# Seven half-size products for each pair of feed-forward up tiles, and the down product as a second pass

## The reference

```
h = rmsnorm(x, g_ffn)
u = h @ w_up                                   # (1024, 1024) @ (1024, 5632)
f_gate = causal_dwconv(u[:, :2816], conv_f_w) + conv_f_b      # 3 taps over tokens
f = gelu(f_gate, tanh) * u[:, 2816:]
x = x + f @ w_down                             # (1024, 2816) @ (2816, 1024)
```

## Time and profile before

| | us |
|---|---|
| median of 3 runs (lowest to highest) | 2121.4 (2120.72 to 2123.34) |
| the profiled execution | 2123.06 |
| its span, first to last instruction | 2121.3 |
| mean granted clock of PE | 0.985 |
| feed-forward part: first up product to last down product | from 619.6 to about 1380 |

### The profile page before, as it was taken

One profiled execution on the slowest core, in us unless ns is written; L12 is line 12 of the kernel. 1 busy time (PEld: TensorE's weight loads), 2 busy tenths in 40 slices (PEclk: granted clock), 3 DMA queues, 4 the chain that ended last, 5 costly groups with the idle time before them and its releaser, 6 DMA issues.

```text
span 2121.3 us, 24908 instructions
## 1 busy us (share of the span) xinstructions
PE 2048.5 (97%) x9765; PEld 1705.9 (80%) x9765; DVE 1177.4 (56%) x1119; ACT 438.5 (21%) x547; POOL 730.0 (34%) x534
## 2 busy tenths in 40 slices
PE   6999999999999999999999999999899999999998
PEld 5888788887887888888888888878788878888877
DVE  4999995313436655566556655744433745556520
ACT  4000001302222000000000000233222235555411
POOL 2444354454232343333433333423122511112221
PEclk9999999999999999999999999999799989999999
DMA  4211111232131112221122112211123210000033
GB/s 134 60 42 48 40 44 45 74 105 60 40 107 52 60 50 80 69 68 38 62 79 69 52 42 74 79 30 40 30 74 95 75 41 1 11 11 1 1 129 90
DMA packets 176851, 122.08 MB, mean 58 GB/s; under 512 B 8771, under 2 KB 160272, under 8 KB 176784
## 3 DMA queue, kind: packets, MB, share of 16 engines
q1 hardware_dynamic: 175504, 118.77, 18.5%
q10 hardware_dynamic: 1280, 2.35, 0.3%
HBM read 112.71 MB, written 8.39 MB: 57 GB/s over the span
## 4 chain that ended last, share of the span: by engine, by line
PE 79%; DVE 7%; issue 4%; POOL 4%; DMA 4%; ACT 3%; SPq 0%; POOLq 0%; DVEq 0%; ACTq 0%
PE ps L488 67%; POOL wlo L437 2%; DMA raw<-in_w_up 2%; PE ps L872 2%; POOL whi L435 1%; DVE prob L1864 1%; PE ps L905 1%; PE ps L886 1%; PE ps L889 1%; PE ps L883 1%; PE ps L907 1%; PE ps L906 1%; PE ps L880 1%; PE ps L892 1%; PE ps L697 1%
## 5 line engine op out<-in xcount | busy, mean ns | idle before, releaser
L437 POOL TENSOR_TENSOR wlo<-raw,whi 128x1024 fp32r<-128x1024 f32 (+2 forms) x162 | 458.4, 2830 | 13.5
L434 POOL TENSOR_TENSOR small<-ones 128x1 f32<-128x1 f32 x166 | 50.7, 306 | 1123.5 <-PE ps L488 928.3
L488 PE MATMUL ps<-xb_hi,whi 128*128 128x512 f32 x1216 | 381.0, 395 | 15.9 <-POOL wlo L437 4.3
L488 PE MATMUL ps<-xa_hi,whi 128*128 128x512 f32 x1184 | 373.8, 395 | 7.6 <-DVE xa_lo L1604 3.1
L488 PE MATMUL ps<-xb_lo,whi 128*128 128x512 f32 x1216 | 376.6, 391 | 0.0
L488 PE MATMUL ps<-xb_hi,wlo 128*128 128x512 f32 x1216 | 376.1, 391 | 0.0
L488 PE MATMUL ps<-xa_lo,whi 128*128 128x512 f32 x1184 | 369.1, 391 | 0.0
L488 PE MATMUL ps<-xa_hi,wlo 128*128 128x512 f32 x1184 | 368.7, 390 | 0.0
L488 PEld LDWEIGHTS ps<-xb_hi,whi 128*128 128x128 f32 x1216 | 227.5, 189 | 70.7 <-issue 9.2
L488 PEld LDWEIGHTS ps<-xb_lo,whi 128*128 128x128 f32 x1216 | 229.6, 189 | 48.6
L488 PEld LDWEIGHTS ps<-xb_hi,wlo 128*128 128x128 f32 x1216 | 229.4, 189 | 48.3
(11 more groups left out here) (323 smaller groups left out, 2247.4 us busy)
## 6 DMA issues: line engine op xcount, KB each, us to landing
raw<-in_w_in SPq DMA_DIRECT2D x52, 512.0 KB, 3.8
raw<-in_w_up SPq DMA_DIRECT2D x44, 512.0 KB, 4.0
raw<-in_w_down SPq DMA_DIRECT2D x22, 512.0 KB, 3.5
w_mod<-in_w_mod SPq DMA_DIRECT2D x40, 256.0 KB, 3.0
x_columns<-in_x SPq DMA_DIRECT2D x8, 512.0 KB, 4.8
raw<-in_w_o SPq DMA_DIRECT2D x8, 512.0 KB, 3.8
raw<-in_w_ple_gate SPq DMA_DIRECT2D x8, 512.0 KB, 3.8
y_scratch<-resid SPq DMA_DIRECT2D x8, 512.0 KB, 3.0
```

The source lines that it names most:

```text
L434: nc.gpsimd.tensor_tensor(small[:, 106 + slab.slot:107 + slab.slot], ones[:, 0:1], ones[:, 0:1], ALU.mult)
L437: nc.gpsimd.tensor_tensor(lo, src, f32(hi), ALU.subtract).then_inc(split_done, 1)
L488: ins = mm(dst[j], w, r[j], start=first and f, stop=last and l)
```

## The change

For 20 of the 22 pairs, the two tiles of a pair are made together. The 2 x 2 blocks are: for the weights, the halves of the 1024 input features (k tiles 0 to 3, 4 to 7) by gate and up tile; for the activations, the same halves of features by the halves of the tokens. Seven products of half size (12 matmuls, one bank each) take the place of eight. What else is done:

- once, ahead of the loop: ACT makes scaled copies of the residual (16 of 128 x 512), DVE four differences of 128 x 2048 (`token_combs`), ACT their rounded parts (`tch`), POOL and DVE two each of the rests (`tcl`)
- per pair: SP loads four quarter slabs (`comb_raw`), DVE makes four sums of weight blocks of 128 x 512 (`weight_sums`), POOL splits seven blocks of 128 x 512 (`comb_split`) in a ring of four places, ACT copies the first product out of PSUM and makes the first tap, DVE adds up the products (`comb_pair`)
- the product with gelu, `f`, goes to a DRAM scratch of 22 x 128 x 1024 (`f_store`) and no down product is made in the loop
- after the loop the down product runs in six chunks of four (the last: two) tiles. SP loads `f` back (`f_load`), ACT rounds it, POOL makes the rest (`f_low`), and the jobs have 24 matmuls. The multiply-adds of `w_mod` and the `ctx` and `p` work move here.

Elsewhere semaphores of DVE's own waits are merged into one (`link`), with the same instructions. The diff, cut:

```diff
+        def comb_raw(i, u, tile_col):
+            for r in range(4):
+                sp.dma_start(raw_part(u, r).rearrange("p (k n) -> p k n", n=P),
+                             w_up[H * (r % 2):H * (r % 2 + 1), ds(tile_col + DFF * (r // 2), P)].rearrange("(k p) n -> p k n", p=P)
+                             ).then_inc(sem(f"st_raw{u % 2}"), 16)
+        def f_store(src, t):
+            sp.wait_ge(sem("f_ready"), t + 1)
+            sp.dma_start(to, src[:, 0:S]).then_inc(sem("f_out"), 16)
...
+        with sp.Fori(0, (PAIRS - 2) // 2) as q:
+            for u in range(2):
+                sp.wait_ge(sem("st_split"), q * 28 + (14 * u + 14))
+                comb_raw(None, u, q * (2 * P) + (4 + u) * P)
+                f_store(T[1], q * 2 + (2 + u))
+        sp.wait_ge(sem("st_split"), 14 * (PAIRS - 1))
+        down_slab(0, 0)
+        down_slab(0, 1)
+        f_store(T[1], NF - 2)
+        sp.wait_ge(sem("f_out"), 16 * (NF - 1))
+        sp.wait_ge(sem("st_done"), 4 + 7 * PAIRS - 3)
+        f_load(0)
+        sp.wait_ge(sem("st_done"), 4 + 7 * PAIRS)
...
+        def comb_split(q, u, n):                                  # POOL
+            g = 7 * u + n
+            cols, s = ring(g % 4)
+            r = (0, 1, None, None, None, None, 3)[n]
+            src = wsum_part((1, 2, 0, 3)[n - 2]) if r is None else raw_part(u, r)
+            pool.wait_ge(sem("st_done"), q * 28 + (g + 1))        # the product four before is done
+            if n == 0:
+                pool.wait_ge(sem(f"st_raw{u % 2}"), q * 128 + 64 * (u // 2 + 1))
+            elif n in (2, 3, 5):
+                pool.wait_ge(sem("st_sum"), q * 16 + (4 * u + {2: 2, 3: 3, 5: 4}[n]))
+            nc.gpsimd.tensor_tensor(small[:, 106 + n % 2:107 + n % 2], ones[:, 0:1], ones[:, 0:1], ALU.mult)
+            nc.gpsimd.tensor_scalar(whi[:, s, cols], src, 1.0, 0.0, ALU.mult, ALU.add).then_inc(sem("st_split"), 1)
+            pool.wait_ge(sem("st_split"), q * 56 + (2 * g + 1))
+            nc.gpsimd.tensor_tensor(wlo[:, s, cols], src, f32(whi[:, s, cols]), ALU.subtract).then_inc(sem("st_split"), 1)
...
+        def combination(q, u, n):                                 # PE, one bank per n
+            if n == 0:
+                pe.wait_ge(sem("st_copied"), q * 4 + (u + 1))
+            else:
+                pe.wait_ge(sem("st_read"), q * 40 + (10 * u + (1, 3, 4, 6, 7, 9)[n - 1]))
+            pe.wait_ge(sem("st_split"), q * 56 + (2 * g + 2))
+            for k in range(4):
+                for i, (wp, bp) in enumerate(((whi, bh), (whi, bl), (wlo, bh))):
+                    last = mm(o, wp[:, s, w], bp[:, k, :], start=k == 0 and i == 0, stop=k == 3 and i == 2)
...
+        def comb_out(q, u):                                       # ACT
+            fn(T[3][:, 0:H], PS[:, 0:H], ACT.Copy).then_inc(sem("st_copied"), 1)
+            gelu(q * 4 + (u + 1))
+            act.wait_ge(sem("st_read"), q * 40 + (10 + 10 * u + 8))
+            fn(T[1][:, 0:S], T[0][:, 0:S], ACT.Identity, scale=dcol("conv_f_w", t), bias=dcol("conv_f_b", t)).then_inc(sem("fc_tap"), 1)
+        with act.Fori(0, PAIRS // 4) as q:
+            for u in range(4):
+                comb_out(q, u)
+        gelu(NF - 1)
+        for c in range(NDC):
+            for k in range(f_tiles(c)):
+                act.wait_ge(sem(f"f_in{2 * (c % 2) + k // 2}"), 16 * (c // 2 + 1))
+                fn(hi[:, k, :], fraw[FSLOT[c]][:, k, :], ACT.Copy).then_inc(sem("f_hi"), 1)
...
+        def weight_sums(q, u):                                    # DVE
+            tt(s1, a21, a22, ALU.add); tt(s2, s1, a11, ALU.subtract); tt(s3, a11, a21, ALU.subtract); tt(s4, a12, s2, ALU.subtract)
+        def comb_pair(q, u, following):                           # DVE; product(k) waits for product k
+            kept, summed = T[3][:, first], T[3][:, second]
+            step(tt(T[0][:, 2:2 + H], product(1), kept, ALU.add))
+            step(tt(T[0][:, 2:2 + H], T[0][:, 2:2 + H], rbc[:, first], ALU.mult))
+            step(tt(summed, product(2), kept, ALU.add))
+            step(tt(kept, product(3), summed, ALU.add))
+            weight_sums(*following)
+            step(tt(T[2][:, second], P5, kept, ALU.add))          # P5 = product(4)
+            step(tt(summed, P5, summed, ALU.add))
+            step(tt(T[0][:, 2 + H:2 + S], product(5), summed, ALU.add))
+            step(tt(T[0][:, 2 + H:2 + S], T[0][:, 2 + H:2 + S], rbc[:, second], ALU.mult))
+            step(tt(T[2][:, first], product(6), kept, ALU.add))
+            step(tt(T[2][:, 0:S], T[2][:, 0:S], rbc[:, :], ALU.mult))
+            taps(t)
+            dve.wait_ge(sem("gelu"), t + 1)
+            tt(T[1][:, 0:S], T[1][:, 0:S], T[2][:, 0:S], ALU.mult).then_inc(sem("f_ready"), 1)
...
+        first_pair(0)                                             # DVE
+        token_combs()
+        token_low()
+        first_pair(1)
+        dve.wait_ge(job_done, JOBS["ffn"] + 4)
+        weight_sums(0, 0)
```

More of the change, by code:

```diff
@@ L336, in mod_rows @@
[L336 to L349, removed]
@@ L352, in sync_program @@
+        for r in range(45, 48):
+            mod_rows(r)
         for u in range(2):
@@ new lines, in tensor_program @@
+        pe.wait_ge(pair_free[0], (Lin(JOBS["ffn"]) + 4).half())
+        pe.wait_ge(pair_free[1], (Lin(JOBS["ffn"]) + 5).half())
+        with pe.Fori(0, PAIRS // 4) as q:
+            for u in range(4):
+                for n in range(7):
+                    combination(q, u, n)
+        J, L = Lin(JOBS["down0"]), Lin(SLABS["down"])
+        pe.wait_ge(pair_free[0], J.half())
+        pe.wait_ge(pair_free[1], J.half())
+        pe.wait_ge(split_done, L.val(1))
+        hi, lo = f_parts(0)
+        pe.wait_ge(sem("st_copied"), PAIRS + 1)
@@ new lines, in tensor_program @@
+        pe.wait_ge(sem("st_read"), 10 * PAIRS + 4)
+        for k in range(4):
+            pe.wait_ge(sem("f_lo"), k + 1)
+            for m in range(2):
+                w = slice(k * 2 * P + m * P, k * 2 * P + m * P + P)
+                last = split_products([pair(J + m, 0, H), pair(J + m, H, S)], whi[:, 0, w], wlo[:, 0, w],
+                                      [hi[:, k, 0:H], hi[:, k, H:S]], [lo[:, k, 0:H], lo[:, k, H:S]], k == 0, k == 3,
+                                      1 if k == 0 and m == 0 else None)
+                if k == 3:
+                    last.then_inc(job_done, 1)
@@ new lines, in first_pair @@
+        def first_pair(t):
+            Jg = Lin(JOBS["ffn"] + 2 * t)
+            dve.wait_ge(job_done, Jg.val(1))
+            tt(T[0][:, 2:2 + S], pair(Jg), rbc[:, :], ALU.mult).then_inc(*one(free(Jg)))
+            dve.wait_ge(*free(Jg))
+            first_tap(t)
+            taps(t)
+            dve.wait_ge(job_done, Jg.val(2))
+            tt(T[2][:, 0:S], pair(Jg + 1), rbc[:, :], ALU.mult).then_inc(*one(free(Jg + 1)))
+            dve.wait_ge(*free(Jg + 1))
+            dve.wait_ge(sem("gelu"), t + 1)
+            tt(T[1][:, 0:S], T[1][:, 0:S], T[2][:, 0:S], ALU.mult).then_inc(sem("f_ready"), 1)
@@ new lines, in vector_program @@
+        dve.wait_ge(sem("cs"), 2)
+        for c in range(NDC - 1):
+            if c == 1:
+                for k in range(2):
+                    J = Lin(JOBS["p"] + k)
+                    dve.wait_ge(sem("pt_hi"), k + 1)
+                    tt(XAl[:, 4 + k, :], pair(J), f32(XAh[:, 4 + k, :]), ALU.subtract).then_inc(*one(free(J)))
+            for m in range(8):
+                down(c, m)
+                if c >= 1:
+                    for r in mod_rows_at(c, m):
+                        g, k = r // 8, r % 8
+                        if k == 4 and g:
+                            read_mod(g - 1)
+                        dve.wait_ge(sem(f"modw_in{r % 2}"), 16 * (r // 2 + 1))
+                        for n in range(2):
+                            mod_mac(k, n, modw[:, r % 2, :], 16 * g + 1, g % 2)
```

437 lines of the change are left out of this document (279 added, 158 removed).

## The result

The changed kernel takes 2164.9 us (median of 4 runs, 2163.9 to 2166.9) against 2121.5 for the kernel before: a ratio of 1.0202, 95% interval 1.0186 to 1.0218. It is 2.0% slower. I had forecast 2133, slower by 0.5%, with 2160 as the upper end: the sign was right, the size was not. The profiled execution has a span of 2162.7 us, 41.4 more than before.

The account below looks back on a forecast made before the run. It took PE to bound the kernel before, and the port shared by POOL and DVE to pace the changed loop. -54.7 + 43 + 14.0 + 9.7 + 1.7, less 2, gave 2133 us, 0.5% slower, range 2098 to 2160.

Parts of the forecast that it names:

- loop over 84 matmuls a pair: Loop over pairs: 21.3 us a pair against PE's 19.15, giving back 43 us over 20 pairs.
- start of the loop: Before the loop: PE waits until both pairs are read, starting at 681.9 instead of 667.9, +14.0 us, between 10 and 18.
- end of the loop: Between loop and down product: PE waits for DVE's last steps, gelu, ACT's rounding and POOL's rest, +9.7 us.
- second pass: Down product after the loop: POOL's splits and rests and the multiply-adds hidden behind PE's 43.8 us per chunk, no cost.
- clock: At the two new waits around the loop: PE's clock drops to the lower level after them, +1.7 us.
- waits of the loop before: Loop of the kernel before: of 2.5 us per turn beyond the products, 0.4 goes in each of five turns, -2 us.
- The port and the loop: Loop: POOL's instructions and DVE's with two SBUF operands exclude each other, setting 21.3 us a pair; chance 0.50.
- the doubt about 19.6 for matmuls into one bank: Loop: PE's pair may take 19.6 us instead of 19.15, since matmuls into one bank start 0.233 us apart.
- The signs: Loop: pairs 21.3 us apart, POOL busy over 90%, its wlo near 2 us on average, DVE's taps over 1.29.
- The clock in the loop: Loop, rival: short pauses of PE lower its clock; two low stretches a pair make 22.6 us, +26, 2159 us; chance 0.04.
- the second pass has waits of its own: Down pass, rival: POOL's rests between slab splits meet DVE's multiply-adds, 2 to 4 us in five chunks, 2148 us; chance 0.10.

Follow-up runs that it names:

- x_psum: Changed kernel with the loop's DVE instructions on two SBUF operands reading PSUM for one of them (values wrong): 2128.4 us, ratio 1.0018 to the kernel before.
- x_act_high: Changed kernel with the loop's rounding moved from POOL to ACT, no tiny instruction, and pair 1's gelu ahead of the copy: 2120.8 us, ratio 0.9971.
- x_macs_psum: Changed kernel with the down pass's multiply-adds reading PSUM bank 6 instead of their rows (values wrong): pass 296.2 us against 318.6, ratio 1.0087.
- x_macs_resident: Changed kernel with the down pass's multiply-adds reading a tile already there, without waiting for row loads (values wrong): pass 310.2 us against 318.6, ratio 1.0131.
- x_columns_later: Changed kernel with the modulation's column products two down jobs later in PE's queue, read two rows later by DVE: 2147.8 us, ratio 1.0116.
- x_four_repairs: Changed kernel with rounding on ACT, running sums in PSUM, a new order at the loop's start and later column products: 2083.2 us, ratio 0.9809.
- x_no_tiny: Changed kernel with POOL's pair loop written out and the one-column instruction ahead of each of 140 roundings left out: 2152.4 us, ratio 1.0123.

## Why the prediction was right in its sign and wrong in its size

The terms of the sum, as predicted and as measured in the changed kernel's trace (us):

| term | predicted | measured | from |
|---|---|---|---|
| products removed | -54.7 | -54.7 | counts |
| loop over 84 matmuls a pair (383.0) | +43 | +41.8 | 424.8 - 383.0 |
| start of the loop | +14.0 | +18.6 | 667.24 to 685.83 |
| end of the loop | +9.7 | +9.8 | 1110.62 to 1120.46 |
| second pass | 0 | +34.1 | 318.6 - 284.5 |
| clock | +1.7 | in the rows above | |
| waits of the loop before | -2 | -6.3 | below |
| elsewhere | 0 | -1.9 | the rest of 41.4 |

The -6.3: from 667.92 to 1396.51 are 728.6 us, less 1920 x 0.228 = 437.8 of up products and the 284.5 of a clean pass. The sum is 41.4 where I had 11.7. That the loop's 41.8 is so near to 43 is in part luck: 43 was the port's price alone, and 9.2 of the 41.8 lie in the first pair (28.3 us against 19.04), which has a gap of 5.1 and the lower clock behind it, and which I hadn't seen. The port took 32.6, since the loop started with a pair at PE's own pace before it settled, and since a steady pair is 21.05 and not 21.3.

**The port and the loop: right.** I forecast 21.3 us a pair, the trace has 21.05; wlo of 512 columns takes 1.26 us by itself (1.31 was my figure), and x_psum and x_act_high show that nothing else held the loop, since both reach PE's own pace. That is 19.04, so the doubt about 19.6 for matmuls into one bank was idle. The signs came out less evenly: POOL was busy for 97%, but its rests were 1.51 on average and not near 2; the roundings (1.03 on average of all) and the tiny instructions (0.47), for which I had named no sign, carried most of the waits. And the opening sentence, that POOL gets more than twice its work per pair, is wrong: the kernel before has three slabs of 3.7 us per pair, 11.1, against 15.4; what fell is PE's time per pair, into which this has to fit, since the down product left the loop. The Trainium skill (GPSIMD Engine Reference, Key points) warns of contention with VectorE instructions of two SBUF inputs, and its SBUF — State Buffer (SBUF: two separate sides) says that the shared pair of ports is an exclusive lock for the whole instruction; the trace agrees, by 1.10 against 0.61 us for the rounding. The Trainium skill's price for a tensor_tensor (GPSIMD Engine Reference, 3.1 Elementwise), an estimate of 1.1 us for 512 columns, is met by no run: the least is 1.26.

**The clock in the loop: right.** PE waits 22.4 us in 18 stops between 716 and 1110, the longest 1.6, and the granted clock is 1.00 there. What I had cited from the Trainium skill (TensorE: Matmul & The Clock Gate, A second HAM failure mode) doesn't show here.

**The end of the loop: right,** 9.8 against 9.7, with the chain as described: gelu, ACT's rounding, POOL's first rest at 1117.80.

**The start: under-sized by 4.6 us, and a second gap of 5.1 that I hadn't seen.** I let the row scales come at 635.9. They came at 641.4, since the broadcast is a step at a fixed place in PE's queue: DVE had its input ready at 633.7, PE reached it at 638.50. The second part is the 5.1 us gap at 692.90, which the loop's figure contains: ACT's queue has the first copy, which waits for PE's product, ahead of gelu of pair 1, and DVE's weight sums are queued behind that gelu. I had followed the start to its first product and no further.

**The second pass: the step that failed.** The sentence was: "the down product has 43.8 us per chunk against POOL's four splits (3.7 each) and four rests (2.4), 24 us: hidden, and so are 12 `w_mod` multiply-adds per chunk." Three things were wrong with it:
- The count. 96 multiply-adds lie in four chunks: 24 per chunk, three behind each down product, not 12.
- The comparison. I set POOL's 24 us against PE alone, although I had found further up that POOL and DVE's two-operand instructions add up. POOL's 24.4 and 24 x 0.74 = 17.8 are 42.2 of 43.8 us: the port has hardly any time left, so each stretch in which the two meet makes DVE late. With the port free 22.4 us of the 34.1 went (x_macs_psum).
- The queues. The rows' loads lie behind 2 MB of `f` in SP's queue (8.4 us alone, x_macs_resident), and the column products stand in PE's queue two jobs behind the sums that they need. Moving only these took 20.4 us off (x_columns_later), and x_four_repairs, with both, has 31.0 less: the two overlap by some 11.

The rival "the second pass has waits of its own" named the place and even the mechanism, POOL's rests with DVE's multiply-adds in the way. It was priced at 2 to 4 us a chunk, 2148, by guess and not from the count; the row at 1273.84 shows 5.5 us at one place. The port's sum for the pass, 42.2 of 43.8, would have forbidden the word "hidden"; by itself it is still under PE's time and doesn't give the 34 us, which come from where the two meet and from what PE's queue asks for next. Some 14 of the 34 us are the clock, which fell behind each of the four waits at L792; my 1.7 counted only the two gaps at the loop's ends.

What stays open: how the 22.4 us of the port divide between POOL's slab roundings and its rests, and why the kernel before lost 6.3 us around its products where I let 2 go.

## What to carry to other kernels

Where two engines share a port, make the sum of both engines' time on it for every stage, moved work included, and compare that with the bound engine; a stage in which each engine looks half idle can be full, and one that is nearly full already loses time where the two meet. What helped here is an instruction that doesn't use the port (one operand or the sum in PSUM, or the work on ACT); another order of the loads or of POOL's rests gave nothing. And ask of each result that another engine's queue needs how far behind its maker it is asked for: two down jobs were too few, four were enough.

## What the runs showed of the hardware that I had not expected

- POOL's one-column instruction is held like a large one: 0.47 us on average in the loop and 0.195 in x_psum; leaving out 7 a pair was worth 0.57 us a pair once the loop ran steadily (x_no_tiny, with POOL's loop written out).
- DVE's multiplication of 512 columns at L1909 took 1.73 to 1.77 us in all 20 pairs, and 0.69 in x_psum: the two queues lock into a fixed rhythm, in which it meets the same instruction of POOL each time, a rest that began 0.07 us before it.
- DVE's multiplication of 512 columns by a column of scales (L1701), with a single operand in SBUF, was held by POOL like those with two: 0.47 to 2.59 us.
- The granted clock was 1.00 in the loop with 22.4 us of waits in 18 stops of at most 1.6, and 0.95 in the pass with 21.9 us of gaps. In the pass it fell behind each of the four gaps at L792 (3.0, 5.5, 6.7 and 2.1 us from one matmul to the next) and not behind one of 2.7 at 1192.02, so the length of a gap doesn't decide it alone. Three matmuls after the 5.1 us gap at 692.90 start 0.43 us apart, where 0.228 is usual:
```profile
698.55 0.63 PE L832 MATMUL ps<-tok_comb_lo,whi 128*128 128x512 f32 x1
698.98 0.63 PE L832 MATMUL ps<-tok_comb_hi,wlo 128*128 128x512 f32 x1
699.41 0.63 PE L832 MATMUL ps<-tok_comb_hi,whi 128*128 128x512 f32 x1
```
